# Sums of the recurrence as 64x64 tiles, far scores of attention one step later, state space products copied out of their bank by ScalarE

## The reference

```python
# first block: state space, 32 groups of 16 channels, 64 complex states each
_, _, x_re, x_im = lax.associative_scan(_complex_affine_combine, (a_re, a_im, bu_re, bu_im), axis=1)
y = einsum('blgp,ghp->blgh', x_re, c_re) - einsum('blgp,ghp->blgh', x_im, c_im) + d * u
# second block: recurrence
w_log = -softplus(-(w0 + tanh(wd) @ w_lora_up)) - 0.5
a = sigmoid(a0 + ad @ a_lora_up)
kk = heads(k * k_k)
kk = kk / maximum(sqrt(sum(kk * kk, axis=-1)), 1e-12)          # sum over the 64 of a head
y = _rwkv7_scan(rh, wh, kh, vh, kk, ah)
mu, var = mean(y, axis=-1), mean(square(y - mu), axis=-1)       # over the 64 of a head
bonus = sum(rh * kh * r_k, axis=-1) * vh                        # over the 64 of a head
# second block: attention, causal and dilated, written here as one masked softmax
s = q @ k.T * hd ** -0.5 + log(number of patterns that allow the pair)
o = exp(s - max(s)) @ v / sum(exp(s - max(s)))
```

## Time and profile before

| | |
|---|---|
| median of 3 executions | 3224.15 us (3223.52 to 3224.88) |
| the profiled execution | 3225.03 us, span 3223.2 us |
| mean granted clock of PE | 0.992 of full |
| busy PE, DVE, ACT, POOL | 3110.9, 1785.2, 1239.8, 160.9 us |
| chain that ended last | PE 81%, DVE 11%, ACT 5%, issue 2%, DMA 1% |

### The profile page before, as it was taken

One profiled execution on the slowest core, in us unless ns is written; L12 is line 12 of the kernel. 1 busy time (PEld: TensorE's weight loads), 2 busy tenths in 40 slices (PEclk: granted clock), 3 DMA queues, 4 the chain that ended last, 5 costly groups with the idle time before them and its releaser, 6 DMA issues.

```text
span 3223.2 us, 56327 instructions
## 1 busy us (share of the span) xinstructions
PE 3110.9 (97%) x23802; PEld 2589.1 (80%) x23802; DVE 1785.2 (55%) x3315; ACT 1239.8 (38%) x2225; POOL 160.9 (5%) x280
## 2 busy tenths in 40 slices
PE   8999999999999999999899999999999899999998
PEld 7888777889878888888677777777777778887886
DVE  7677543374772343435773556565546756566443
ACT  5224433333542221213452423444444434445332
POOL 1011000010000000000010000000001300000000
PEclk9999999999999999999999999999999999999999
DMA  4212132144322111124354322001004322224643
GB/s 143 80 61 94 53 119 80 52 138 159 116 96 71 53 43 53 39 64 129 104 209 131 121 80 90 27 18 37 25 2 150 130 93 79 79 86 138 204 126 120
DMA packets 102091, 297.48 MB, mean 92 GB/s; under 512 B 13280, under 2 KB 13408, under 8 KB 101712
## 3 DMA queue, kind: packets, MB, share of 16 engines
q1 hardware_dynamic: 83568, 237.21, 22.5%
q0 software_dynamic: 12944, 37.32, 3.3%
q10 hardware_dynamic: 5328, 19.34, 1.5%
HBM read 233.75 MB, written 57.94 MB: 90 GB/s over the span
## 4 chain that ended last, share of the span: by engine, by line
PE 81%; DVE 11%; ACT 5%; issue 2%; DMA 1%; POOL 0%; SPq 0%; DVEq 0%; ACTq 0%; POOLq 0%
PE ps L129 67%; PE ps L128 12%; DVE w_lo L168 1%; ACT w_hi L165 1%; PE ps L137 1%; DVE HB L168 1%; DVE HB L178 1%; DVE C L178 1%; ACT a_PT L165 1%; ACT m_D L147 1%; DVE ssm_Dop L188 1%; DVE m_SS L178 0%; ACT L152 0%; DVE n L178 0%; DVE a_A L182 0%
## 5 line engine op out<-in xcount | busy, mean ns | idle before, releaser
L168 DVE TENSOR_TENSOR w_lo<-w_raw,w_hi 128x1024 fp32r<-128x1024 f32 (+3 forms) x354 | 374.0, 1057 | 406.3 <-ACT w_hi L165 404.9
L129 PE MATMUL ps<-XHA,w_hi 128*128 128x264 f32 (+3 forms) x1456 | 466.6, 320 | 10.7 <-DVE w_lo L168 5.5
L129 PE MATMUL ps<-XLA,w_hi 128*128 128x264 f32 (+3 forms) x1456 | 456.8, 314 | 0.0
L129 PE MATMUL ps<-XHA,w_lo 128*128 128x264 f32 (+3 forms) x1456 | 454.9, 312 | 0.0
L165 ACT ACTIVATE w_hi<-w_raw 128x1024 fp32r<-128x1024 f32 (+3 forms) x354 | 323.9, 915 | 294.2 <-PE ps L129 206.4
L129 PE MATMUL ps<-XHB,w_hi 128*128 128x512 f32 x920 | 370.1, 402 | 6.9 <-DVE w_lo L168 4.3
L129 PE MATMUL ps<-XLB,w_hi 128*128 128x512 f32 x920 | 360.2, 392 | 0.0
L129 PE MATMUL ps<-XHB,w_lo 128*128 128x512 f32 x920 | 360.1, 391 | 0.0
L129 PEld LDWEIGHTS ps<-XHA,w_hi 128*128 128x128 f32 x1456 | 275.1, 189 | 39.5 <-issue 14.1
L129 PEld LDWEIGHTS ps<-XLA,w_hi 128*128 128x128 f32 x1456 | 275.1, 189 | 21.2 <-issue 3.6
L129 PEld LDWEIGHTS ps<-XHA,w_lo 128*128 128x128 f32 x1456 | 275.6, 189 | 16.5
(11 more groups left out here) (444 smaller groups left out, 5944.1 us busy)
## 6 DMA issues: line engine op xcount, KB each, us to landing
w_raw<-in_f_gate SPq DMA_DIRECT2D x50, 512.0 KB, 3.3
w_raw<-in_f_up SPq DMA_DIRECT2D x50, 512.0 KB, 3.3
w_raw<-in_f_down SPq DMA_DIRECT2D x64, 384.0 KB, 3.2
w_raw<-in_w_out SPq DMA_DIRECT2D x32, 512.0 KB, 3.3
w_raw<-in_w_rkv SPq DMA_DIRECT2D x24, 512.0 KB, 3.3
w_raw<-in_w_attn SPq DMA_DIRECT2D x24, 512.0 KB, 3.9
h<-HB POOLq DMA_DIRECT2D x40, 256.0 KB, 2.5
hid<-C POOLq DMA_DIRECT2D x18, 512.0 KB, 2.9
```

Of the source, the lines that this page charges most:

```text
L129: return Issued(e.matmul(out, a, b, start=start, stop=stop))
L168: return Issued(self.eng and self.eng.tensor_tensor(out, a, b, op))
```

## The change

Four things, and a few lines that they need:

1. ACT copies the 256 columns of `("k", j)` into `ssm_q1` at once, and that frees the bank. DVE makes its 16 copies from `ssm_q1`, in SBUF, after that.
2. `dense64` makes two products of 64 rows and 64 columns, one for each head, into the same bank.
3. The two LoRA products become four of 64x64, with no wait between them. Both read all 64 rows of the shared activations; the weights have 32 rows of zeros in the half that doesn't belong. The second weight tile `K.al` lies in a part of `HB`, so SP waits for the stores of `h2` before it loads it, and ACT waits for all LoRA products before it writes attention's result there.
4. `scores(u, c0)` makes one chunk. PE makes the far chunk a step after the near one; DVE does the same for the first unit of a block.

```diff
@@ ssm_act
-        yield from pause(9)
+        yield
+        A.wait_ge(S.pe, ("k", j))
+        A.cp(K.ssm_q1[:, 0, :], K.sb["k", j][:, 0:256]).then_inc(S.act, ("k", j))
+        K.sb.done(("k", j), S.act, ("k", j))
+        yield from pause(8)
@@ ssm_dve
-        V.wait_ge(S.pe, ("k", j))
+        V.wait_ge(S.act, ("k", j))
         V.wait_ge(S.pool, "dz")
-        b = K.sb["k", j]
+        b = K.ssm_q1[:, 0, :]
...
-        K.sb.done(("k", j), d, ("D", j))
@@ in3_sp
-            D.dma(K.wl[:, :], K.I["lora_wa"]).then_inc(K.lora, by=16)
+            for sig in K.hs:
+                D.wait_ge(sig, ("h2", 1))
+            D.dma(K.wl[:, :], K.I["lora_w"]).then_inc(K.lora, by=16)
+            D.dma(K.al, K.I["lora_a"]).then_inc(K.lora, by=16)
@@ rwkv_pe
         def dense64(name, b, lhs, src, sig, event):
             P.wait_ge(sig, event)
-            P.mm(b, lhs, src, True, True).then_inc(S.pe, (name, u))
+            for h in range(2):
+                op = P.mm(b[heads(h), :], lhs[heads(h), heads(h)], src[heads(h), :], True, True)
+            op.then_inc(S.pe, (name, u))
...
-        P.mm(low(b), K.wl[0:32, 128 * j:128 * j + 128], tokens(K, u, slice(0, 32)), True, True).then_inc(S.pe)
-        P.after(S.pe)
-        P.mm(high(b), K.wl[32:64, 128 * j:128 * j + 128], tokens(K, u, slice(32, 64)), True, True).then_inc(S.pe, ("la", u))
+        for half, weights in ((low(b), K.wl), (high(b), K.al)):
+            for h in range(2):
+                op = P.mm(half[heads(h), :], weights[:, 128 * j + 64 * h:128 * j + 64 * h + 64], tokens(K, u, slice(0, 64)),
+                          True, True)
+        op.then_inc(S.pe, ("la", u))
@@ attention_pe
-        def scores(u):
+        def scores(u, c0):
             i = BLOCKS[u // 2]
-            chunks = [(c0, min(512, 128 * (i + 1) - c0)) for c0 in range(0, 128 * (i + 1), 512)]
-            banks = [[ps.take(P, ("s", j, u + h, c0)) for c0, _ in chunks] for h in range(2)]
-            for n, (c0, cn) in enumerate(chunks):
+            cn = min(512, 128 * (i + 1) - c0)
+            if cn > 0:
+                banks = [ps.take(P, ("s", j, u + h, c0)) for h in range(2)]
                 for h in range(2):
-                    P.mm(banks[h][n][:, 0:cn], K.aq[heads(h), 128 * i:128 * i + 128], K.ak[heads(h), c0:c0 + cn], True,
+                    P.mm(banks[h][:, 0:cn], K.aq[heads(h), 128 * i:128 * i + 128], K.ak[heads(h), c0:c0 + cn], True,
                          True).then_inc(S.pe, ("s", j, u + h, c0))
...
-                scores(u)
+                scores(u, 0)
                 yield
+                scores(u, 512)
@@ attention_act, values(i)
             A.wait_ge(S.pe, ("w", j, i))
+            if j == 3 and i == 4:
+                for T in K.rws:
+                    A.wait_ge(T.pe, ("la", 3))
@@ attention_dve
                 for c0 in range(0, n, 512):
                     cn = min(512, n - c0)
+                    if c0 and not h:
+                        yield
...
-                yield
+                if h or i < 4:
+                    yield
@@ make_memory
+        K.al = K.HB[0:64, 7, 512:1024]
@@ layout
-    o["lora_wa"] = np.concatenate([g["w_lora_up_2"], g["a_lora_up_2"]], axis=0)
+    none = np.zeros_like(g["w_lora_up_2"])
+    o["lora_w"] = np.concatenate([g["w_lora_up_2"], none], axis=0)
+    o["lora_a"] = np.concatenate([none, g["a_lora_up_2"]], axis=0)
```

## The result

The changed kernel takes 3181.28 us (median of 4 runs, 3180.36 to 3183.53), the kernel before 3224.52 us beside it (4 runs): ratio 0.9866, 95% interval 0.9851 to 0.9881, 43.2 us less. The forecast of 3187 us was 5.7 us too high; the time lies in the range. A second comparison gave 0.9859 (0.9843 to 0.9876). The profiled execution took 3183.53 us with a span of 3181.7 us, 41.5 less than before.

A forecast was written before the change was run, and what follows sets the result against it. PE was taken to set the pace in both the state space and the recurrence and attention stages. Terms -14.4 - 13.2 - 4.9 - 14.8 + 3.6 + 6 = -37.7 us, from 3225.0 to 3187 us; range 3177 to 3205.

The forecast's parts named there:

- State space, -14.4: State space stage: three PE waits for copies into ssm_Dop (9.7 us) and lower clock behind two (4.7) go.
- The rival that the gaps come back elsewhere: State space stage: the removed gaps return at other places, so the 14.4 us are lost: 3201 us; chance 0.10.
- Changes of tile shape, -13.2 and +3.6: LoRA through attention: 80 fewer shape changes at 0.165 us save 13.2; moving far scores adds 22, costing 3.6.
- LoRA, -4.9: LoRA products: the uncovered wait between each pair's two products goes, about 0.30 us in 16 places, 4.9 us less.
- The rival with tiles one after the other: LoRA products: 64x64 tiles on the same rows don't run side by side, 14 us more: 3201 us; chance 0.08.
- Two row halves into one bank: Sums: rival that two row halves can't write one bank together, 28 us more: 3215 us; chance 0.03.
- a_PT, -14.8: Attention: far scores a step later remove PE's waits for ACT's a_PT copies (15.4 us), 14.8 us less.
- The return, +6: Attention: DVE's far minimum and ACT's exponential, now nearer PE's far scores, delay stream copies; 6 us more, bounds 0 to 48.
- What would show it: Profile signs, including no ssm_Dop wait, LoRA group 0.87 us, a_PT wait near 1 us, stage 20 to 28 us shorter.
- the lower end of the range: Whole kernel: all gains without return give 3181 us; a little more if each shape change is worth 0.2: 3177.

The follow-up runs named there:

- e2: Kernel before, with idle PE products in the two long state space gaps (j = 0 and j = 3), nothing moved: 3224.12 us, ratio 0.9991.
- e4: Kernel before with only the LoRA products changed to four 64x64 tiles, with the loads and waits they need: 3217.66 us, ratio 0.9972.
- e6: Changed kernel with the far scores put back beside the near ones, other three edits kept: 3195.16 us, ratio 0.99 to the kernel before.
- e5: Kernel before with only the far scores one step later, on PE and DVE: 3213.02 us against 3227.86, ratio 0.9955.
- e8: Changed kernel with far scores and DVE's far minimum two steps later instead of one: 3196.5 us, ratio 0.9904 to the kernel before.
- e7: Changed kernel, but DVE takes the far minimum right behind the near one, as before: 3196.12 us, ratio 0.99 to the kernel before.
- e10: Changed kernel run again, unaltered, on the same chip as a version with idle products: 3182.74 us, ratio 0.9859 to the kernel before.

## Why the prediction was right, and where its sizes were off

- **State space, -14.4:** right, 14.5 in the whole change and 14.2 alone. The clock was measured apart, 4.6 us at the end of this stage (e2), which leaves 9.9 for the gaps (9.7). At the end of the kernel e2 keeps only 2.8 by the medians. The rival that the gaps come back elsewhere is refuted for the stage; 1.3 us of the whole change are given back before the first LoRA product, for a reason that no run shows.
- **Changes of tile shape, -13.2 and +3.6:** right in kind. The net of 58 changes at 0.165 is 9.6 us; the whole change shows 28.0 - 13.3 of waits - 4.9 for LoRA = 9.8. The single edits give 0.14 (sums), 0.16 (LoRA, if its wait is 4.9), 0.13 and 0.11 (far scores). One microsecond between two traces is 0.05 for each of 21 changes, so these don't show that the price differs from place to place; they show some 0.11 to 0.17.
- **LoRA, -4.9:** right only as seen together with its 24 changes: the edit gave 8.6 us (e4), 8.9 by the prediction. The 4.9 alone isn't shown. The rival with tiles one after the other is refuted by 0.91 us for the four.
- **Two row halves into one bank:** 0.44 us for the pair of 256 columns, 0.87 if one after the other. The Trainium skill, TensorEngine Tiling (Array Packing), Restrictions and Gotchas (Gotcha 1: PSUM Pressure), says that different row tiles can't access one bank at the same time. The measurement disagrees, here for tiles that write different partitions of the bank, and decides.
- **a_PT, -14.8:** 13.9 (15.4 to 1.5), and e6 brings it back whole.
- **The return, +6: this is the mis-sized term.** The prediction took "about twice the largest group of today" for PE's waits behind ACT and DVE. Measured, PE's waits other than for a_PT go from 7.2 to 7.8 us in the whole change, +0.6, of which the load of `a_k` is 1.3, and by -0.6 in e5. With +0.6 the prediction's own sum is -43.1 us, or 3182. A row of before pointed that way: ACT already waited for minima up to 3.0 us in 48 places while PE's waits for the streams stayed below 3 us in each group, and after the change ACT's longest is 3.2. That this is why nothing came back is argued; e8, with waits of 5.8 to 8.3 us, fits it. The price was not false in kind, though: it comes at once if DVE's minimum does not move along (e7) or if it moves two steps (e8), 11.4 and 13.0 us of the stage. Of the steps tried, that of the change is the one where both are covered.
- **The whole:** the four parts measured one by one give 12.2 + 8.7 + 9.2 + 14.8 = 44.9 us by the medians, the whole 43.2 and 44.1. By the stretches, where less noise comes in, they give 14.2 + 7.0 + 8.6 + 11.8 = 41.6, the whole 14.5 + 28.0 = 42.5. Within what the runs can tell they add up, and no part needs another.
- **Slips that change nothing:** 16 x 0.30 is 4.8, not 4.9; and with 0.2 for each of the 58 changes the lower end of the range comes to 3179, not 3177.
- **What would show it:** the listed signs are there, with a_PT at 1.5 us instead of near 1 and the LoRA group at 0.91 instead of 0.87. The stretch from the first a_V transposes to the last squares is 26.2 us shorter (439.4 to 413.2).

## What to carry to other kernels

Where PE is busy for 94% of a stage, count what it does between instructions: each change of tile shape cost some 0.11 to 0.17 us here, and cutting a product to the shape of its neighbours paid though its columns stay the same. When a product is moved to a later step, move what reads its result on the next engine by as much. Then look at the waits of every in-order engine in between, the longest one (it told in e8, for ACT) as well as their number and sum, and at whether PE asks for what stands behind them. In e7 DVE's longest wait was that of the changed kernel and 11.4 us were lost all the same, so the longest wait alone is no safe sign. Before filling gaps for the sake of the clock, see whether PE is what ends the stretch behind them, and whether the filling can start before the wait ends.

## What the runs showed of the hardware

- 64x64 fp32 tiles on the same rows and different columns go side by side (4 products of 256 columns in 0.91 us), as do tiles on different rows that write one bank (2 in 0.44 us).
- DVE's copies of 32 partitions by 256 to 160 columns take 282 to 238 ns out of SBUF, by the group means below, where they took 372 ns in the median out of the bank; ACT's copy of all 256 columns takes 382 ns. Groups of the changed kernel (count, then busy us and mean ns):

```profile
L188 DVE COPY ssm_Dop<-ssm_q 32x256 f32<-32x256 f32 x16 | 4.5, 282 | 14.6 <-ACT ssm_q L165 14.3
L188 DVE COPY ssm_Dop<-ssm_q 32x160 f32<-32x160 f32 x16 | 3.8, 238 | 0.5
L165 ACT ACTIVATE ssm_q<-ps 128x256 f32<-128x256 f32 x4 | 1.5, 382 | 1.3 <-PE ps L128 1.3
```

- The same gap of PE is followed by the lower clock in one execution and not in another (0.89 and 1.00 over 455 to 470), which is 15 x 0.11 = 1.7 us at this place. The four executions of the changed kernel in e10 lie between 3179.7 and 3185.1.
